# Attention on one Trainium2 core: scores in three single PSUM banks with half-width exponentials, and four rotating work banks for the small products

## The reference, cut to what matters

```python
# A: 8 query heads, 2 kv heads, head_dim 64; latent tokens see 256 cached keys + their own 1024
s = jnp.einsum('bkgqd,bksd->bkgqs', qb, k).astype(jnp.float32) * scale
p = jax.nn.softmax(s, axis=-1).astype(v.dtype)
return jnp.einsum('bkgqs,bksd->bkgqd', p, v)
...
# B: 4 heads, two halves of 32 dims each, value dim 64
s1 = jnp.einsum('bhqd,bhsd->bhqs', qb[..., :B_QK_DIM], k1).astype(jnp.float32) * scale
s2 = jnp.einsum('bhqd,bhsd->bhqs', qb[..., B_QK_DIM:], k2).astype(jnp.float32) * scale
a = jax.nn.softmax(s1, axis=-1) - lam32 * jax.nn.softmax(s2, axis=-1)
return jnp.einsum('bhqs,bhsd->bhqd', a.astype(v.dtype), v)
```

## Time and profile before

| | |
|---|---|
| median of 3 runs | 2575.77 us (2574.27 to 2577.35) |
| the profiled execution | 2577.81 us, its span 2576.1 us |
| PE busy | 2280.4 us (89%) |
| DVE, ACT, POOL busy | 1454.9, 912.6, 886.1 us |
| mean granted PE clock | 0.938 |
| weight loads of the work products (L1151) waiting for DVE maxima (L1344) | 147.0 us, 288 times |
| exponentials (L1284) waiting for scores | 359.6 us (A) and 321.1 us (B) |

### The profile page before, as it was taken

One profiled execution on the slowest core, in us unless ns is written; L12 is line 12 of the kernel. 1 busy time (PEld: TensorE's weight loads), 2 busy tenths in 40 slices (PEclk: granted clock), 3 DMA queues, 4 the chain that ended last, 5 costly groups with the idle time before them and its releaser, 6 DMA issues. The chain is left out here.

```text
span 2576.1 us, 29010 instructions
## 1 busy us (share of the span) xinstructions
PE 2280.4 (89%) x10853; PEld 1553.9 (60%) x10853; DVE 1454.9 (56%) x2351; ACT 912.6 (35%) x1530; POOL 886.1 (34%) x486
## 2 busy tenths in 40 slices
PE   4799999879999999968958999989899999999698
PEld 3578987655455545427736889876554455555276
DVE  5677100866655666576556770008666656666865
ACT  5432212423444434432154322124244444434321
POOL 0212210415555555551002121114255655555510
PEclk9999999879999999989978999999799999999799
DMA  7332221011011101014373322220111011100233
GB/s 247 107 111 82 66 76 49 13 45 30 12 30 30 30 20 27 18 49 123 114 246 102 111 82 66 76 56 7 45 30 29 13 30 30 30 18 19 80 117 98
DMA packets 234454, 165.21 MB, mean 64 GB/s; under 512 B 162684, under 2 KB 187712, under 8 KB 234304
## 3 DMA queue, kind: packets, MB, share of 16 engines
q1 hardware_dynamic: 234304, 163.26, 21.9%
HBM read 124.80 MB, written 38.42 MB: 63 GB/s over the span
## 5 line engine op out<-in xcount | busy, mean ns | idle before, releaser
L1284 ACT ACTIVATE probs<-scores 128x1024 f32<-128x1024 f32 x320 | 326.4, 1032 | 680.7 <-PE scores L1170 359.6
L1108 POOL TENSOR_TENSOR prob_sums<-prob_sums,probs 128x1024 f32<-128x1024 f32 x208 | 500.4, 2406 | 184.7 <-ACT probs L1284 169.3
L1344 DVE TENSOR_REDUCE neg_max_parts<-work 128x1 f32<-128x512 f32 (+1 forms) x608 | 391.6, 687 | 292.4 <-PE work L1151 287.5
L526 POOL TENSOR_TENSOR w_lo<-w_stage,w_hi 128x512 fp32r<-128x512 f32 (+1 forms) x112 | 134.9, 1236 | 827.3 <-ACT w_hi L461 827.3
L428 PE MATMUL z_acc<-w_hi,h_hi 128*128 128x512 f32 (+1 forms) x640 | 237.8, 372 | 12.3 <-DVE h_lo L545 8.1
L428 PE MATMUL z_acc<-w_lo,h_hi 128*128 128x512 f32 (+1 forms) x640 | 235.2, 367 | 0.0
L428 PE MATMUL z_acc<-w_hi,h_lo 128*128 128x512 f32 (+1 forms) x640 | 235.1, 367 | 0.0
L1105 POOL TENSOR_TENSOR prob_sums<-probs 128x1024 f32<-128x1024 f32 x32 | 76.1, 2378 | 411.5 <-ACT probs L1284 411.5
L850 DVE MEMSET k_stackB<- 128x24 f32 (+1 forms) x4 | 0.9, 218 | 346.6 <-PEq L312 346.6
L1187 PE MATMUL att_out<-probs,vB 128*64 128x512 f32 x640 | 186.6, 703 | 3.1 <-DVE oa L1364 3.1
L428 PE MATMUL z_acc<-h_hi,w_lo 128*128 128x512 f32 (+1 forms) x528 | 187.0, 354 | 0.0
(11 more groups left out here) (248 smaller groups left out, 4258.6 us busy)
## 6 DMA issues: line engine op xcount, KB each, us to landing
mod_w<-in_w_mod SPq DMA_DIRECT2D x24, 1024.0 KB, 7.3
w_stage<-in_w_in SPq DMA_DIRECT2D x96, 256.0 KB, 3.1
z_scratch<-z_out SPq DMA_DIRECT2D x60, 256.0 KB, 2.0
cv<-u_scratch SPq DMA_DIRECT2D x20, 512.0 KB, 6.4
u_scratch<-z_out SPq DMA_DIRECT2D x32, 256.0 KB, 2.0
out_y_sample<-y_tiles SPq DMA_DIRECT2D x16, 512.0 KB, 5.1
k_rawA<-z_scratch SPq DMA_DIRECT2D x16, 320.0 KB, 4.1
q_rawA<-z_scratch SPq DMA_DIRECT2D x16, 320.0 KB, 4.4
```

The source lines that it names most:

```text
L526: pool.tensor_tensor(w_lo[:, n % RING, 0:cols], stage[:, n % STAGES, 0:cols], w_hi[:, n % RING, 0:cols].bitcast(F32), ALU.subtract).then_i ...
L1108: ins = pool.tensor_tensor(a, a, pr[:, n % NPB, :], ALU.add)
L1284: act.activation(pr[:, n % NPB, :], sc[n % 2][:, :, :].rearrange("p c n -> p (c n)"), ACT.Exp, scale=SCALE[u]).then_inc(s["a_exp"], 1)
L1344: dve.tensor_reduce(dst, src, AX_X, ALU.max, negate=True).then_inc(s["a_wkdve"], 1)
```

## The change

Four things change in `attention_block`:

1. The scores use three single banks in rotation. Half c of step i is chunk `chunk(p, i, c)`; it waits for the exponential of three chunks earlier. ACT takes each chunk with its own exponential of 512 columns; the prompt step is one chunk, both its key tiles in one bank.
2. `att_sums` is gone. Four work banks rotate over all pieces, the prompt part of `weigh` (use 18 of a unit) and `sums` (the last use). Use x waits until use x - 4 has been read (`work_bank`, `wait_read`).
3. Pieces 27 to 29 are copied out by ACT (`stand`), after the last exponential of the unit, no longer by DVE.
4. `DIRECT` is 1 for both kinds: a B unit sums its next to last key tile on POOL too, and its `sums` has one source less. The first unit's maxima go through the work banks, 512 columns at a time, like those of all others.

```diff
-DIRECT = {"A": 1, "B": 2}
+DIRECT = 1
+SCORE_BANKS, WORK_BANKS = 3, 4
+CHUNKS = 2 * KT_S + 1
+USES = PREP + 2
+PROMPT_USE = 18
...
-        sc = [ctx.enter_context(nc.psum_tensor(f"scores{i}", [P, 2, NB], F32)) for i in range(2)]
+        sc = [ctx.enter_context(nc.psum_tensor(f"scores{i}", [P, NB], F32)) for i in range(SCORE_BANKS)]
         ob = ctx.enter_context(nc.psum_tensor("att_out", [P, NB], F32))
-        sm = ctx.enter_context(nc.psum_tensor("att_sums", [P, NB], F32))
-        wk = [ctx.enter_context(nc.psum_tensor(f"work{i}", [P, NB], F32)) for i in range(2)]
+        wk = [ctx.enter_context(nc.psum_tensor(f"work{i}", [P, NB], F32)) for i in range(WORK_BANKS)]
...
+        def prep_use(p, i):
+
+            return i if p == 0 else PREP + USES * (p - 1) + i + (1 if i >= PROMPT_USE else 0)
+
+        def prompt_use(p):
+            return PREP + USES * p + (PROMPT_USE if p < UNITS - 1 else 0)
+
+        def sums_use(p):
+            return PREP + USES * p + (USES - 1 if p < UNITS - 1 else 1)
...
+        def work_bank(eng, x):
+            if x >= WORK_BANKS:
+                wait_read(eng, x - WORK_BANKS)
+            return wk[x % WORK_BANKS]
...
-                bank = wk[i % 2]
-                if i < 2:
-                    if p:
-                        pe.wait_ge(s["a_wkdve"], DVE_PIECES * p - 1 + i)
-                elif i < PREP_MAX:
-                    pe.wait_ge(s["a_wkact"], PREP_MAX * p + i - 1)
-                elif i < PREP_MAX + 2:
-                    pe.wait_ge(s["a_wkact"], PREP_MAX * (p + 1))
-                else:
-                    pe.wait_ge(s["a_wkdve"], DVE_PIECES * p + i - 1 - PREP_MAX)
+                bank = work_bank(pe, prep_use(p, i))
+                if i == PREP_MAX:
+                    wait_read(pe, prep_use(p, PREP_MAX - 1))
...
-            def scores(p, i):
+            def scores(p, i, c):
                 u, h = of_unit(p)
-                n = p * STEPS + i
-                if n >= 2:
-                    pe.wait_ge(s["a_exp"], n - 1)
-                if i == 0:
-                    pe.wait_ge(s["a_wkdve"], DVE_PIECES * (p + 1))
+                m = chunk(p, i, c)
+                if m >= SCORE_BANKS:
+                    pe.wait_ge(s["a_exp"], m - SCORE_BANKS + 1)
+                if i == 0 and c == 0:
+                    wait_read(pe, prep_use(p, PREP - 1))
+                bank = sc[m % SCORE_BANKS]
...
             def sums(p):
-                pe.wait_ge(s["a_pout"], p + 1)
+                bank = work_bank(pe, sums_use(p))
...
             def exps(p, i):
...
-                    act.activation(pr[:, n % NPB, :], sc[n % 2][:, :, :].rearrange("p c n -> p (c n)"), ACT.Exp,
+                for c in range(1 if i == PROMPT_AT else 2):
+                    m = chunk(p, i, c)
+                    act.wait_ge(s["a_scores"], m + 1)
+                    act.activation(pr[:, n % NPB, c * NB:(c + 1) * NB], sc[m % SCORE_BANKS][:, :], ACT.Exp,
...
+                        if i == LAST:
+                            for x in range(PREP_LAST, PREP):
+                                stand(nxt, x)
...
-                for i in range(PREP_LAST, PREP):
-                    cols = slice((i - PREP_LAST) * NB, min((i - PREP_LAST + 1) * NB, TOK))
-                    dve.wait_ge(s["a_work"], PREP * p + i + 1)
-                    dve.tensor_copy(qT2[u][:, cols], wk[i % 2][:, 0:cols.stop - cols.start]).then_inc(s["a_wkdve"], 1)
```

More of the change, by code:

```diff
@@ L1187, in weigh @@
                         mm = pe.matmul(ob[rows, :], v[u][:, j, :], probs[:, q], start=(j == 0), stop=(j == KT_S - 1))
+                    mm.then_inc(s["a_pv"], 1)
                 else:
+                    bank = work_bank(pe, prompt_use(p))
                     for what in range(2):
-                        for c in range(2):
+                        for k in range(2):
                             for rows, q in halves(P):
[L1192 to L1195, removed]
+                                lhs = per["ones"][:, :] if what else v[u][:, KT_S + k, :]
+                                mm = pe.matmul(bank[rows, what * P:(what + 1) * P], lhs,
+                                               probs[:, k * SEQ + q.start:k * SEQ + q.stop], start=(k == 0), stop=(k == 1))
+                    mm.then_inc(s["a_pv"], 1)
             def sums(p):
-                u, h = of_unit(p)
-                pe.wait_ge(s["a_pout"], p + 1)
-                sources = []
+                bank = work_bank(pe, sums_use(p))
                 for j in range(summed(p), KT_S):
[L1202 to L1206, removed]
+                    last = pr[:, (p * STEPS + TILE_AT.index(j)) % NPB, :]
                     for rows, q in halves(NB):
-                        mm = pe.matmul(sm[rows, :], per["ones"][:, :], src[:, q], start=(x == 0), stop=(x == len(sources) - 1))
+                        pe.matmul(bank[rows, :], per["ones"][:, :], last[:, q], start=(j == summed(p)), stop=False)
+                pe.wait_ge(s["a_add"], adds(p, LAST))
+                for rows, q in halves(NB):
+                    mm = pe.matmul(bank[rows, :], per["ones"][:, :], acc[:, p % 2, q], start=False, stop=True)
                 mm.then_inc(s["a_sum"], 1)
@@ L1214, in pieces, with ahead @@
                         prep(p, i)
+            def ahead(p, i):
+                for c in range(1 if i == PROMPT_AT else 2):
+                    scores(p, i, c)
             def run_unit(p):
@@ L1219, in run_unit @@
                     pieces(nxt, 6 * g, 2)
-                    scores(p, GROUPS[g + 1][0])
+                    ahead(p, GROUPS[g + 1][0])
                     pieces(nxt, 6 * g + 2, 2)
-                    scores(p, GROUPS[g + 1][1])
+                    ahead(p, GROUPS[g + 1][1])
                     pieces(nxt, 6 * g + 4, 2)
@@ L1226, in run_unit @@
                 pieces(nxt, 24, 2)
-                scores(p, LAST)
+                ahead(p, LAST)
                 pieces(nxt, 26, 1)
@@ L1235, in run_unit @@
                     for i in GROUPS[0]:
[L1236 to L1249, removed]
+                        ahead(nxt, i)
+            for i in range(PREP):
                 prep(0, i)
             for i in GROUPS[0]:
-                scores(0, i)
+                ahead(0, i)
             for p in range(UNITS):
@@ L1267, in stand @@
                 else:
-                    cols = slice((i - PREP_Q) * NB, min((i - PREP_Q + 1) * NB, TOK))
-                    ins = act.copy(qT[u][:, cols], bank[:, 0:cols.stop - cols.start])
+                    g = i - (PREP_Q if i < PREP_MAX else PREP_LAST)
+                    cols = slice(g * NB, min((g + 1) * NB, TOK))
+                    dst = qT if i < PREP_MAX else qT2
+                    ins = act.copy(dst[u][:, cols], bank[:, 0:cols.stop - cols.start])
                 ins.then_inc(s["a_wkact"], 1)
@@ L1318, in run_unit @@
                         split_hi(u, h + 1)
-            for i in range(PREP_MAX):
-                stand(0, i)
+            for i in range(PREP):
+                if i < PREP_MAX or i >= PREP_LAST:
+                    stand(0, i)
             for p in range(UNITS):
```

73 lines of the change are left out of this document (40 added, 33 removed).

## The result

The changed kernel takes 2453.42 us (median of 4 runs, 2450.77 to 2454.97), the one before 2575.78 in the same session: a ratio of 0.9524 (95% interval 0.9507 to 0.954), 122 us faster. I had forecast 190 us, 2386, with a range up to 2440: right in sign, and too low even for its range. The profiled execution took 2454.1 us; its span is 2452.5 and its mean granted clock 0.949.

The account below looks back on a forecast made before the run. PE was taken as the bound, held up by two work banks, ACT at B starts and a falling clock. Pairs 183, first units 7.6, starts 4, last units -4.8: 190 us gained, so 2386, range 2350 to 2440.

Parts of the forecast that it names:

- DVE's pace: Rival: DVE's maxima still set the pace of PE's bursts, so only 67 us are gained, 2509; chance 0.05.
- Wait for the last maxima 0.15: New B unit: PE waits 0.15 us for the last maxima, within a forecast unit of 29.2 us.
- 0.4 for the wait on the last maxima and on the prompt output: New A unit: 0.4 us added for both waits to a sum of 30.5, giving 30.9 us.
- 0.232 us for every matmul: Bursts in both units: each 512 column matmul takes 0.232 us unheld, making 10.9 us in A and 7.9 in B.
- The B start: Start of a B unit: set by ACT's 7.87 us of work, 8.5 us in all against 10.9 before.
- ring waits: B unit: half chunks wait for the exponential three before; three close meetings at 0.1 make 0.3 us.
- the lower bound that I took: Half exponentials on ACT: two cost 0.03 us more than one wide; upper bound 0.59 each without overlap.
- Copies on ACT: Unit end: about 1.3 us of copies moved to ACT, hidden behind PE's last `weigh` and sums of 2.7 us.
- POOL not the bound: Both units: POOL's eight additions take 19.3 us, under unit lengths of 29.2 and 30.9.
- The last unit: Last unit of each layer: POOL's last addition ends the chain, one more costs 2.4 us, twice, a 4.8 loss.
- The clock did not fall in B: Rival claimed the clock still falls in B units, 2.7 us each, so 2424, at most 2459; chance 0.28.
- three score banks tie PE to ACT: Slower rival: each of ten steps waits if ACT answers late; 2610 at 0.7 us a step; chance 0.04.

Follow-up runs that it names:

- three reductions: Changed kernel with the small copy of the last maxima and the subtraction behind it written as three DVE reductions: 2410.3 us, ratio 0.9364 to the kernel before.
- the copy alone replaced: Changed kernel with the copy of the last maxima written as a one-element reduction, the subtraction kept: 2437.97 us, ratio 0.9471 to the kernel before.

## Why the prediction was right in kind and wrong in size

- **What bounds the kernel** was read rightly: PE, held up by two work banks and by a clock that fell behind waits. Banks give the gain (137 us from two to three), the clock in every B unit stays at 1.00, and DVE's pace rules no burst but the one behind the prompt output in B, for which 1.1 us had been allowed.
- **The step that failed** is "Wait for the last maxima 0.15" in B, and in A the "0.4 for the wait on the last maxima and on the prompt output". It measured 0.81 to 0.97 in B and 1.34 in A for the maxima, and twice in seven A units the clock fell behind it. In the trace that I worked from POOL was idle at that moment in B units and held the copy for some 0.4 us in A. The change put the copy deeper under POOL's additions: in A by the new times alone, in B by the new times and POOL's added addition together. It cost 43 us (41 by the ratios), 37 of them in the fourteen pairs, shown by taking it away.
- **The mis-sized term** is 0.232 us for every matmul. It comes from 48 matmuls of one form in a row; the bursts have changes of form on both sides. In A they were forecast at 2.8, 3.25, 3.25 and 1.63 us, and measured 2.98, 3.47, 3.61 and 1.84 with three reductions; in B, where 2.1, 2.3, 3.4 and 1.2 were forecast, 2.27, 2.62, 3.50 and 1.37. Transposes had 1.25 for 1.05. With 0.35 more at the start of B, and less the 0.85 of waits that I had allowed (0.4, 0.15, 0.3) and that are then gone, this makes up 1.6 of the 1.7 us a pair, 24 in all. That one more change of form costs time was shown (0.34 us a block); how it divides over the places of a unit was read, not tested.
- **The B start** (8.85 for 8.5), its ring waits, `weigh` at full pace and ACT without a gap were right. The half exponentials pace at the lower bound that I took: in ACT's timeline after, four take 2.07 us; less 0.61 for the last, that is 0.49 for each of three.

```profile
597.49 2.07 ACT L1310 ACTIVATE probs<-scores 128x512 f32<-128x512 f32 x4 [2.55 <-PE scores L1204]
```

- **Copies on ACT**: nothing, right. **POOL not the bound**: right as a sum, wrong as a conclusion: it was no bound, and still held DVE. **The last unit**: the size was right (2.45 us for 2.4) by luck, since POOL's addition makes only 0.5 to 1.1 of it, as shown above.
- **Rivals.** The clock did not fall in B, but it fell in two of seven A units, where I had not looked. The rival that ends slower (three score banks tie PE to ACT) did not come.

## What to carry to other kernels

When a change makes the critical engine earlier, look at what the other engines do at the new times: a short DVE step that ran beside an idle POOL may then run under its operations, and in this kernel a copy or a two-input operation on SBUF was held to their end, where a reduction was not. A step that takes 0.18 us in some units and 0.6 in others, in the trace of before, is the sign to look for. Price matmuls by rows with the same neighbours, not by a long uniform run, and put spare blocks of work where an engine's answer is due rather than behind a burst. Count banks by what each gives, and see what else a run with one bank less changes: here the third was worth 137 us, while the 9 us of the fourth hid the cost of the held copy. Before splitting buffers, look for a bank that is kept for a rare use and could join them.

## What the runs showed of the hardware that I had not expected

- A DVE copy of 128 x 10 elements, 0.18 us alone, took up to 1.88 us beside a running POOL addition of 2.4 us; a subtraction with both inputs in SBUF did the same (medians of 0.97 and 1.67), a reduction of the same size never (0.17).
- A block of 64 column matmuls put between 128 column ones cost 0.34 us more than the same matmuls next to another such block.
- An idle stretch of PE of 1.34 us before ten small transposes was followed by a lower clock in two of seven units and not in the others (0.95 and 1.00 over the unit), with the same instructions. With the copy alone replaced, the stretch was 1.13 us and a lower clock followed in none.
